# Expert tiles by token rank: two or four experts side by side in TensorE's column groups, 24 tiles in place of 32

## The reference

```python
def _hier_moe(x, rg_w, rg_b, re_w, re_b, w1, w3, w2):
    pg = softmax(x @ rg_w + rg_b)                # 4 groups, the best one is taken
    pg_top, g_idx = top_k(pg, 1)
    le_sel = (x @ re_w + re_b) of that group     # 8 experts, the best two are taken
    v2, i2 = top_k(softmax(le_sel), 2)
    gate = pg_top * v2 / sum(v2)                 # for the two chosen experts
    h = silu(x @ w1[e]) * (x @ w3[e])            # 1024 -> 256, twice
    y += (h * gate) @ w2[e]                      # 256 -> 1024
```

## Time and profile before

| | us |
|---|---|
| median of 3 runs (1572.84 to 1576.59) | 1576.01 |
| profiled execution | 1573.97 |
| its span, first to last instruction | 1572.1 |
| routing and its set-up | 1090.6 to 1130.1 |
| expert tiles, first gather to last second product | 1131.8 to 1507.3 |
| final block, to the end | 1519.7 to 1572.1 |
| mean granted TensorE clock | 0.933 |

### The profile page before, as it was taken

One profiled execution on the slowest core, in us unless ns is written; L12 is line 12 of the kernel. 1 busy time (PEld: TensorE's weight loads), 2 busy tenths in 40 slices (PEclk: granted clock), 3 DMA queues, 4 the chain that ended last, 5 costly groups with the idle time before them and its releaser, 6 DMA issues. The chain is left out here.

```text
span 1572.1 us, 34886 instructions
## 1 busy us (share of the span) xinstructions
PE 1379.3 (88%) x14852; PEld 1190.6 (76%) x14852; DVE 674.7 (43%) x1344; ACT 444.2 (28%) x910; POOL 523.8 (33%) x439
## 2 busy tenths in 40 slices
PE   7898879999999999999999997675499999999930
PEld 6787669789789889889889886564498888888820
DVE  2659543453453453454354344553522222222237
ACT  2152224234234234234234223220012222121224
POOL 2515452371371371371372372320011211112116
PEclk9999889999999999999999997696599999999975
DMA  9958148638638738737736733702849898999745
GB/s 273 251 161 268 58 127 248 197 103 242 209 96 237 222 96 232 227 96 231 229 96 201 219 100 107 53 21 96 299 153 326 310 323 298 323 331 319 274 181 241
DMA packets 278735, 317.31 MB, mean 202 GB/s; under 512 B 20028, under 2 KB 258184, under 8 KB 277296
## 3 DMA queue, kind: packets, MB, share of 16 engines
q1 hardware_dynamic: 262232, 275.77, 57.0%
q0 software_dynamic: 10576, 22.86, 3.9%
q10 hardware_dynamic: 5792, 16.70, 3.5%
HBM read 300.13 MB, written 31.87 MB: 211 GB/s over the span
## 5 line engine op out<-in xcount | busy, mean ns | idle before, releaser
L1438 PE MATMUL psum<-arena 128*128 128x256 f32 (+3 forms) x1536 | 310.1, 355 | 3.6 <-DMA arena<-in_w_in 3.6
L1438 PEld LDWEIGHTS psum<-arena 128*128 128x128 f32 x1536 | 255.7, 193 | 35.0 <-DMA arena<-in_w_in 3.8
L2213 PE MATMUL psum<-arena 128*128 128x128 f32 x2048 | 235.0, 275 | 0.0
L2213 PEld LDWEIGHTS psum<-arena 128*128 128x128 f32 x2048 | 232.5, 192 | 0.5 <-issue 0.5
L1150 DVE COPY_PREDICATED arena<-arena,psum 128x128 f32<-128x128 int32 x280 | 84.2, 301 | 140.4 <-PE psum L1621 133.5
L1434 PE MATMUL psum<-arena 128*128 128x128 f32 x1152 | 139.2, 280 | 4.2 <-DVE arena L1018 4.2
L601 POOL TENSOR_TENSOR arena<-arena 128x768 f32<-128x768 f32 (+1 forms) x32 | 58.9, 1841 | 248.0 <-ACT arena L811 248.0
L1434 PEld LDWEIGHTS psum<-arena 128*128 128x128 f32 x1152 | 134.7, 196 | 6.8 <-issue 6.4
L1396 PE MATMUL psum<-arena 64*64 64x64 f32 x3264 | 119.9, 226 | 13.9 <-ACT arena L822 10.6
L1396 PEld LDWEIGHTS psum<-arena 64*64 64x64 f32 x3264 | 107.8, 140 | 31.3 <-ACT arena L822 14.8
L2086 POOL DMA_INDIRECT y_d<-arena x32 | 32.1, 1002 | 288.3 <-PE psum L2202 135.8
(11 more groups left out here) (361 smaller groups left out, 2061.6 us busy)
## 6 DMA issues: line engine op xcount, KB each, us to landing
arena<-in_w_in SPq DMA_DIRECT2D x96, 1024.0 KB, 6.4
arena<-in_exp_w SPq DMA_DIRECT2D x96, 1024.0 KB
arena<-in_w_out SPq DMA_DIRECT2D x32, 1024.0 KB, 6.0
arena<-in_w_in SPq DMA_DIRECT2D x24, 512.0 KB, 5.4
arena<-y_d SPq DMA_DIRECT2D x8, 1024.0 KB, 12.8
arena<-in_x_prompt ACTq DMA_DIRECT2D x15, 512.0 KB, 4.4
arena<-in_w_in SPq DMA_DIRECT2D x8, 576.0 KB, 5.2
out<-arena POOLq DMA_DIRECT2D x9, 512.0 KB, 3.0
```

Source lines behind the costliest of these rows:

```text
L1438: ins = mm(b[:, 0:n], hT[:, c, :], w[:, c, 0:n], start=(c == 0), stop=(c == KC - 1))
L2213: ins = mm(bank[2 + u % 2][:, j * P:(j + 1) * P], w13[u][:, c, j * P:(j + 1) * P], xT[u % 2][:, c, :], start=(c == 0), stop=(c == KC - 1))
```

## The change

An expert's place is now its rank by token count, found on the chip. Experts 0 to 3 are given the first four ranks, so that their weights can be loaded before the ranks are known. Of the 32 ranks the first 12 have room for 128 rows, the next 8 for 96, the last 12 for 64. Tiles still have 128 slots ("quads"), but each holds parts of two experts (64 slots each) or four (32 each):

- kind H, six times: two experts, two tiles, each with 64 slots of both;
- kind L, six times: two experts, one tile;
- kind M, twice: four experts, three tiles, the middle one with 32 slots of each.

That makes 24 tiles, in the order of SEQUENCE. A rank over its room goes to further tiles as before.

The two operands of the first product change places: the rows (`xT`) are stationary, 64 or 32 columns wide, and the 512 columns of w1 and w3 stream. The hidden values then come out with the rows on the partitions and are transposed (`turn_h`) and copied (`put_hT` on VectorE) ahead of the second product, which is split in the same way. There are six weight buffers in place of four. Loads take the expert's number from a table of ranks through a register. The hardware loops are gone; all 24 turns are written out. Transposes are issued two tiles ahead in place of one. The gates are computed behind the table in place of ahead of the one-hot rows. All eight full x2 tiles (six before) and the final norm's weights are loaded at the end of the expert block.

```diff
-CAP = 128
+TS, NB, AT_ONCE, PACK = 32, 6, 4, 4096
+N4, N3, N2 = 12, 8, 12
+SEQUENCE = "HHHLHLMLHLMLHL"
+def place_experts():
+    quads, first, second, rank_of = [], {}, {}, []
+    ranks = {"H": 0, "M": N4, "L": N4 + N3}
...
+    for kind in SEQUENCE:
+        n, count = len(rank_of), 4 if kind == "M" else 2
+        rank_of += range(ranks[kind], ranks[kind] + count)
+        ranks[kind] += count
+        if kind == "M":
+            rows((n, 64), (n + 1, 64))
+            rows((n, 32), (n + 1, 32), (n + 2, 32), (n + 3, 32))
+            rows((n + 2, 64), (n + 3, 64))
+        else:
+            for _ in range(2 if kind == "H" else 1):
+                rows((n, 64), (n + 1, 64))
...
+LAST_QUAD = [max(q for q, parts in enumerate(QUADS) if n in [p[2] for p in parts]) for n in range(N_EXP)]
...
@@ routing stage, TensorE
-            mm(bank[0][:, 0:(NTT + 1) * 32], cum, S, start=True, stop=False, skip_group_check=True)
-            for t in range(NTT):
-                ins = mm(bank[0][:, (t + 1) * 32:(NTT + 1) * 32], ones,
+            mm(bank[0][:, 0:NTT * 32], cum, S, start=True, stop=False, skip_group_check=True)
+            pe.wait_ge(step("run"), 1)
...
+            mm(bank[6][0:32, 0:32], ones[0:32, 0:32], above[0:32, :], start=True, stop=True).then_inc(step("rank_mm"), 1)
...
             for n in range(T2):
                 pe.wait_ge(step("hot"), n // (T2 // 3) + 1)
-                ins = mm(bank[3][:, 0:TILES], slot_hot[:, n * P:n * P + P], tile_hot[:, n * TILES:n * TILES + TILES],
-                         start=(n == 0), stop=(n == T2 - 1))
+                j = n % 2
+                ins = mm(bank[4][64 * j:64 * j + 64, 0:P], tile_hot[:, 64 * n:64 * n + 64], slot_hot[:, n * P:n * P + P],
+                         start=(n < 2), stop=(n >= T2 - 2))
...
@@ routing stage, VectorE
+            for t in range(NTT):
+                then(tt(run[:, 32 * t + 32:32 * t + 64], run[:, 32 * t:32 * t + 32], S[:, 32 * t:32 * t + 32], ALU.add))
...
+            v.scalar_tensor_tensor(key_row[F, :], bank[1][F, 64:96], 32.0, key_lead[F, :], ALU.mult, ALU.add)
...
+            ts(above[F, :], key_row[F, :], key_col[F, :], None, ALU.is_lt).then_inc(step("above"), 1)
...
+            v.tensor_copy(by_rank[0:1, :], bank[6][0:1, 64:96]).then_inc(step("by_rank"), 1)
...
@@ loads, SP
+    def load_ranked(sp, n):
+        hold(sp)
+        e = sp.value_load(by_rank[0:1, RANK_OF[n]:RANK_OF[n] + 1], min_val=0, max_val=N_EXP - 1)
+        load_from(sp, e, n % NB, weights_in(n % NB))
...
-            def body(e, u):
-                after(sp, "mm2", e)
-                hold(sp)
-                load_w(sp, e + NW, u, weights_in(u))
...
+            for n in range(NB, N_EXP):
+                sp.wait_ge(step("mm2"), LAST_QUAD[n - NB] + 1)
+                load_ranked(sp, n)
+            for n in range(N_EXP - NB, N_EXP - 2):
+                sp.wait_ge(step("mm2"), LAST_QUAD[n] + 1)
+                for t in (2 * (n - N_EXP + NB), 2 * (n - N_EXP + NB) + 1):
+                    sp.dma_start(x2[t], x2_d[t * P:t * P + P, :]).then_inc(step(f"x2_in{t}"), 16)
+            sp.dma_start(fg, A["final_norm_g"].partition_broadcast(P)).then_inc(step("fg_in"), 16)
...
@@ expert stage, TensorE
-                for j in range(4):
-                    for c in range(KC):
-                        ins = mm(bank[2 + u % 2][:, j * P:(j + 1) * P], w13[u][:, c, j * P:(j + 1) * P],
-                                 xT[u % 2][:, c, :], start=(c == 0), stop=(c == KC - 1))
+                for at, width, n in QUADS[q]:
+                    pe.wait_ge(weights_in(n % NB), 48 * (n // NB + 1))
+                for c in range(KC):
+                    for at, width, n in QUADS[q]:
+                        ins = mm(bank[2 + q % 2][at:at + width, :], xT[q % 2][:, c, at:at + width],
+                                 w13[n % NB][:, c, :], start=(c == 0), stop=(c == KC - 1))
...
+            def turn_h(q):
+                after(pe, "h", q)
+                for c in range(2):
+                    ins = tr(bank[2 + q % 2][:, c * P:c * P + P], h[:, c * P:c * P + P], ident)
+                ins.then_inc(step("hidT_mm"), 1)
...
                 for b in range(2):
                     for c in range(2):
-                        ins = mm(bank[4 + 2 * (u % 2) + b][:, :], hT[u % 2][:, c * P:(c + 1) * P],
-                                 w2[u][:, c, 512 * b:512 * b + 512], start=(c == 0), stop=(c == 1))
+                        for at, width, n in QUADS[q]:
+                            ins = mm(bank[4 + 2 * (q % 2) + b][at:at + width, :], hT[q % 2][:, c * P + at:c * P + at + width],
+                                     w2[n % NB][:, c, 512 * b:512 * b + 512], start=(c == 0), stop=(c == 1))
...
+            transposes(0)
+            transposes(1)
+            for q in range(NQ):
+                mm1(q)
+                if q:
+                    mm2(q - 1)
+                turn_h(q)
+                if q + 2 < NQ:
+                    transposes(q + 2)
+            mm2(NQ - 1)
```

More of the change, by code:

```diff
@@ new lines, in experts @@
+    slot_hot = borrow(T2 * P)
+    oh, tmp = borrow(T2 * 32), borrow(T2 * 32)
+    S = xT_flat[1][:, 0:NTT * 32]
+    run = xT_flat[1][:, 320:320 + (NTT + 1) * 32]
+    lg = xT_flat[1][:, 640:640 + NTT * 36].rearrange("p (t n) -> p t n", n=36)
+    places, fold = xT_flat[0][:, 0:P], xT_flat[0][:, P:P + 64]
+    first_b, second_b, ovT, ovT_b = (xT_flat[0][:, 192 + P * n:192 + P * n + P] for n in range(4))
+    key_row, above, of_rank, key_lead, ahead = (xT_flat[0][:, 704 + 32 * n:736 + 32 * n] for n in range(5))
@@ new lines, in _ @@
+            dve.wait_ge(step("of_rank"), 1)
+            then(tt(above[F, :], of_rank[F, :], iota[F, 0:32], ALU.mult))
+            red(ex_col[F, :], above[F, :], AX, ALU.add).then_inc(step("ex_col"), 1)
+            dve.wait_ge(step("pos_mm"), 1)
+            for k in range(2):
+                then(tt(tmp.rearrange("p (t k e) -> p t k e", k=2, e=32)[:, :, k, :], oh4[:, :, k, :],
+                        t3(bank[0][:, 0:NTT * 32], 32), ALU.mult))
+            then(red(pos, tmp3, AX, ALU.add))
@@ new lines, in _ @@
+            ts(parts_i[:, 0:2 * T2], uw_i, PACK - 1, None, ALU.bitwise_and)
+            then(ts(parts_i[:, 2 * T2:4 * T2], uw_i, PACK.bit_length() - 1, None, ALU.logical_shift_right))
+            then(v.tensor_copy(parts, parts_i))
+            first, second, cap32, ovb = (parts[:, n * T2:n * T2 + T2] for n in range(4))
+            ts(far, pos, float(2 * TS), None, ALU.is_gt)
+            then(tt(step_up, second, first, ALU.subtract))
+            v.scalar_tensor_tensor(over, cap32, float(TS), pos, ALU.mult, ALU.is_lt)
@@ new lines, in _ @@
+            tt(tile3, tile3, bcast(dst_f, 64), ALU.mult)
+            for third in range(3):
+                N = slice(third * T2 // 3, (third + 1) * T2 // 3)
+                tt(slot3[:, N, :], bcast(iota, T2 // 3, 1), bcast(place[:, T2 + N.start:T2 + N.stop], P), ALU.is_equal
+                   ).then_inc(step("hot"), 1)
+            dve.wait_ge(step("over_mm"), 1)
+            then(v.tensor_copy(ov_end, bank[7][:, 0:32]))
+            then(tt(ov_end, bank[7][:, 32:64], ov_end, ALU.subtract))
@@ new lines, in _ @@
+            dve.wait_ge(step("places_mm"), 1)
+            v.tensor_copy(places, bank[4][:, 0:P]).then_inc(step("places"), 1)
+            for b in range(OVER // 8):
+                then(tt(ov_le, bcast(ov_end, 8, 1), bcast(iota[:, 8 * b:8 * b + 8], 32), ALU.is_le))
+                then(red(ov_exp[:, 8 * b:8 * b + 8], ov_le, AX, ALU.add))
+            then(v.tensor_copy(ov_exp[:, OVER:OVER + 1], bank[7][:, 64:65]))
+            then(v.tensor_copy(ov_exp_i, ov_exp))
+            dve.wait_ge(step("table_mm"), 1)
@@ L1951, in _ @@
+            then(ts(table_f, bank[5][:, 0:TILES], float(NONE), None, ALU.add))
+            then(v.tensor_copy(table, table_f))
+            then(ts(tokens, table, 1, None, ALU.logical_shift_right))
             dve.wait_ge(step("e4"), 1)
@@ L2019, in _ @@
[L2019 to L2049 removed]
+            then(tt(gate_v[:, :, 1], mx, m2, ALU.mult))
@@ L2103, in _ @@
+            scatter(NQ - 1)
+            for b in range(NX):
+                pool.wait_ge(step(f"y_out{b}"), 16 * (NQ // NX))
         @block.scalar
@@ L2192, in _ @@
+            put_y(NQ - 1)
         @block.tensor
```

515 lines of the change are left out of this document (259 added, 256 removed).

## The result

| | before | after |
|---|---|---|
| median of four runs each | 1576.3 us | 1563.72 us (1562.33 to 1565.79) |
| ratio, 95% interval | | 0.992 (0.9901 to 0.9939) |
| profiled execution | 1573.97 us | 1564.52 us |
| its span | 1572.1 us | 1562.7 us |
| moved by DMA | 317.31 MB | 317.40 MB |

The change takes 12.6 us off, inside the forecast range, but a little under half of the 26 us that were forecast against the median. In the profiled execution it is 9.4 us where 24 were forecast.

The account below looks back on a forecast made before the run. TensorE bounds the kernel, DMA right behind; after the change DMA paces the stage. 1144.4 + 281 + 0.7 + 44.5 + 2.5 = 1473, plus 10 clock = 1483, plus 64.8 and 1.9: 1550 us; forecast 1532 to 1570, chance 0.78.

Parts of the forecast that it names:

- period of a tile: TensorE, expert stage: transposes 0.88, first product 6.87, second 3.43, hidden-row transposes 0.22, switches 0.28; 11.7 us with full pairing.
- waits for weights: TensorE idle for expert weights at tiles 10, 11, 14, 17, 18 and 21: 44.5 us in sum.
- hence 1144.4: First product's start in the expert stage: 1140.7 before, plus 3.7 us for a later stage begin; bounds 2 and 8.
- nothing else queues behind SP there: Weight refills on SP: 3.0 us from a buffer's release to flow, with no other work queued behind SP.
- The walk: Tile-by-tile costing of the expert stage's 24 tiles: first product at 1144.4, 44.5 us of weight waits, end 1473 before clock falls.
- 355 GB/s: DMA rate for a full mixture of weights and rows, bounds 340 and 368; 8.9 us per expert, 2.0 us of rows per tile.
- 7 us of rests: DMA's short rests in the expert stage from 1182 on, beside 272 us of transfer; expert 31 lands at 1463.
- The walk's sample: Expert 13's transfer starts after eight others since 1182 (71 us) and lands at 1267.7; tile 10 is ready at 1262.1.
- rivals 1 and 2: (1) Column groups pair only in part: 1582 us, chance 0.06. (2) No pairing, period 22: 1783 us, chance 0.03.
- The clock's price: TensorE, expert stage: five waits over 3 us let the clock fall, about 2 us each, 10 in all.
- 0.7 + 2.5: Stage edges on TensorE: 0.7 us first activation uncovered, 2.5 us last second product less the transposes no longer there.
- an empty stretch before it: Sign to look for: an empty DMA stretch before 1182, from which on DMA's share is over 1.

Follow-up runs that it names:

- The first two runs: Changed kernel with experts 4 and 5 loaded at the expert block's head: 1562.57 us; the same, but only after the third gather landed: 1559.22 us.
- the split refill: Changed kernel with each buffer's w1 and w3 refilled after the first product of its last tile, w2 after the second: 1528.96 us.
- the third experiment: Changed kernel with the loop over column groups outside the chunks in both products, so groups run one after the other: 1694.98 us, one run.
- split refills, late loads and order: Changed kernel with w1/w3 refilled after the first product, experts 4 and 5 loaded after the third gather, and SEQUENCE HHLHLHMMLHLHLL: 1510.19 us.
- late loads: Changed kernel with experts 4 and 5 loaded at the expert block's head, only once the third gather has landed: 1559.22 us.
- the first experiment: Changed kernel with experts 4 and 5 loaded at the head of the expert block instead of inside the routing block: 1562.57 us.

## Why the prediction was right and wrong

The profiled execution took 14.5 us more than the 1550 forecast, and the gain was under half of the forecast one. By the prediction's own steps:

| step | forecast | measured |
|---|---|---|
| period of a tile | 11.7 | 11.70 |
| first gather | about 1135.5 | 1141.43 |
| gather to first transposes | 4.54 (as before) | 8.48 |
| first product | 1144.4 | 1154.63 |
| waits for weights | 44.5 in six tiles | 48.5 in eight |
| last second product ends | 1483 | 1498.1 |
| from there to the span's end | 64.8 | 64.7 |

**The step that failed is the stage's start, "hence 1144.4".** It took the way from the table to the first product over from before, 10.2 us too short. Of these, 1.2 are a later routing block (1091.8 against 1090.6), 0.5 the routing's own work (43.7 us where 39.5 + 3.7 were forecast; VectorE waited 2.2 us for the last place matmuls, not 1.3, and the forecast's terms add to 28.3 us, not 28.5), 4.2 SP, which stood in the issues of experts 4 and 5 while the barrier waited, 3.9 the gather beside those loads, and 0.4 the way from the transposes to the first product. The prediction did let experts 4 and 5 "land by 1151" and gave this no price. In its "nothing else queues behind SP there" it looked at refills only; the barrier between the blocks is what queued behind SP. It priced an issue by the first of three alone (0.56 us), while the trace of before already had others of nearly 4 us in the routing block:

```profile
1095.62 3.86 SPq L1840 DMA_DIRECT2D arena<-in_exp_w  x1
```

The first two runs put numbers on both terms at the first product: 3.6 and 3.9 us. At the end they are worth less as long as buffers are released late: of 4.7 and 7.6 us, 1.2 and 3.5 arrive. Only with the split refill does the whole arrive.

**The walk held, 4.8 us short.** From first product to last second product it gave 338.6 us and the trace has 343.4: 4.0 of this are longer waits, 0.8 the rest. It named tiles 10, 11, 14, 17, 18 and 21, which are the tiles with pauses over 2 us; sizes were off by up to 4 (13.1 against 9.3 at tile 14, 3.8 against 8.0 at tile 11), so the nearly right sum is partly luck. 355 GB/s was a fair price, a little low: full stretches show 368 and 374 at shares of 1.05 and 1.06. The 7 us of rests were too few: the share is 0.87 from 1320 to 1360 and 0.85 from 1400 to 1440. The walk's sample miscounts in words: expert 13 has seven refills ahead of it, and its 71 us hold its own transfer too.

**Pairing is full, so rivals 1 and 2 fall.** The pairs 7 ns apart and the period of 11.70 us show it; the third experiment shows what the interleaving is worth. The figure of the Trainium skill in "TensorE: Matmul & The Clock Gate", section "Measured speedup vs the span model", 2.38x for three column tiles, does not carry over to this stream: here two groups give 13.7/6.92 = 1.98x, and four 27.5/7.0 = 3.9x.

**The clock's price held.** The first product takes 8.4 to 9.2 us instead of 6.92 at the five tiles with the longest pauses (10, 11, 14, 18, 21), 9 us more in sum, where 10 was set. The stretch 1154.6 to 1163.4 shows a mean granted clock of 0.80, part of it at 1.2 and part at 2.4 GHz; ahead of the transposes TensorE had done nothing for 19.24 us.

**Why a large gain came out small.** 367 - 281 = 86 us left TensorE's path. 48.5 us came back as waiting for weights and about 10 as fallen clocks; the other 4 or so I put down to the stage's edges, where less overlaps (the prediction had 0.7 + 2.5 there). That leaves the 23 us that the traces show between first and last product (343.4, before 1507.3 - 1140.92 = 366.4). The start takes 13.7 of these back (1154.63 against 1140.92), and the stage's end moved by 9.3. Most of the waiting did not need more bandwidth to go: split refills, late loads and order take the waits to 7.0 us with the same bytes. The prediction had "an empty stretch before it" in its list of signs, but counted it as given; with the release that causes it, it was the largest term within reach.

Left open: the longer pause at tile 18 with late loads, and why the routing block's start differs between programs with the same trunk (1087.3 to 1092.8 in these traces).

## What to carry to other kernels

When a change turns a stage from compute-bound to transfer-bound, look for the last time the transfer engines stand empty before they are full: bytes moved there cost the compute engine nothing here, and when a buffer is released (per operand, not per tile) and in which order tiles consume buffers decide how many there are. Here the split refill took 35.6 us off the stage and the order 13.9. Cost a transfer issued ahead of a barrier twice: once for the time its issue holds the issuing engine, once for what it takes from the first transfer behind the barrier. Put the loop over column groups inside the loop over chunks.

## What was not expected of the hardware

- **An issue can hold its engine for microseconds.** Of an expert's three issues of 1024 KB the first is short even beside full DMA (0.57 us at 1131.83), and the second and third are long when another expert's load went out just before: 3.01 and 3.81 us here, 6.73 in the first experiment. With DMA nearly empty (1190.54) the three take 0.55, 0.61 and 1.46 us; the next load, 4 us later, shows it again:

```profile
1195.28 5.62 SPq L1914 DMA_DIRECT2D arena<-in_exp_w  x1
```

- **TensorE takes instructions ahead across column groups**, some four deep (third experiment). The Trainium skill says in "TensorEngine Tiling (Array Packing)", section "Key Properties", that tiles operate independently, with loads and matmuls in parallel; this trace agrees, and adds that it needs no interleaved order at the edges between groups, but does in between.
- **The place matmuls pair too**, with 128 streamed columns: their 36 passes stand in pairs 6 to 7 ns apart, 0.213 us from pair to pair at a granted clock of 0.50, and take 4.1 us, before 7.92. Before, single passes also stood 0.213 us apart at that clock, but streamed 49 columns against 128 stationary ones, so the two times do not compare the same work.
- **The first gather takes 4.54 us to the transposes without weight loads beside it and 8.48 beside two experts' loads**, with DMA at a share of 1.07.
